# Seven half-sized products in place of eight for the gate groups of three feed-forwards

## What is computed

```python
def first_block(x, ...):
    for l in range(DEPTH):                       # DEPTH = 2
        x = x + 0.5 * swiglu(rmsnorm(x, norm_ffn1[l]), w_ffn1_in[l], w_ffn1_out[l])
        x = x + mixing_sublayer(rmsnorm(x, norm_mix[l]), ...)
        x = x + 0.5 * swiglu(rmsnorm(x, norm_ffn2[l]), w_ffn2_in[l], w_ffn2_out[l])
    return rmsnorm(x, norm_final)
# second block, at its end:
        x = x + jnp.square(jax.nn.relu(hm @ w_mlp_in)) @ w_mlp_out
```

## Time and profile before

| | us |
|---|---|
| time, median of 3 runs | 3125.79 (3125.71 to 3126.05) |
| span of the profiled execution | 3124.5 |
| TensorE busy | 3108.5 |
| VectorE busy | 1536.1 |
| ScalarE busy | 1097.2 |
| GpSimd busy | 253.3 |

### The profile page before, as it was taken

One profiled execution on the slowest core, in us unless ns is written; L12 is line 12 of the kernel. 1 busy time (PEld: TensorE's weight loads), 2 busy tenths in 40 slices (PEclk: granted clock), 3 DMA queues, 4 the chain that ended last, 5 costly groups with the idle time before them and its releaser, 6 DMA issues.

```text
span 3124.5 us, 35882 instructions
## 1 busy us (share of the span) xinstructions
PE 3108.5 (99%) x14334; PEld 2531.9 (81%) x14334; DVE 1536.1 (49%) x2472; ACT 1097.2 (35%) x1536; POOL 253.3 (8%) x223
## 2 busy tenths in 40 slices
PE   9999999999999999999999999999999999999998
PEld 7888887788888888888877788888888877888887
DVE  6434436565443444344456555434556555564352
ACT  5323335333322332233344333322456433332222
POOL 0000104102000010000022011000201000110001
PEclk9999999999999999999999999999999999999999
DMA  5333322222433233333222233233332333333332
GB/s 155 95 96 97 131 88 68 75 81 95 140 96 96 91 105 95 101 95 115 95 75 68 69 105 110 95 95 97 105 107 78 97 96 100 101 95 95 101 94 74
DMA packets 95044, 302.01 MB, mean 97 GB/s; under 512 B 11088, under 2 KB 21456, under 8 KB 94300
## 3 DMA queue, kind: packets, MB, share of 16 engines
q1 hardware_dynamic: 94880, 299.73, 30.8%
HBM read 297.54 MB, written 5.29 MB: 97 GB/s over the span
## 4 chain that ended last, share of the span: by engine, by line
PE 99%; DMA 0%; DVE 0%; ACT 0%; issue 0%; SPq 0%; POOL 0%; POOLq 0%; ACTq 0%; DVEq 0%
PE bank L1657 93%; PE score_ps L1483 1%; PE out_ps L1516 1%; PE turn_ps L1494 1%; PE out_ps L1535 1%; PE score_ps L1525 1%; PE score_ps L1557 1%; PE score_ps L1607 0%; PE turn_ps L1503 0%; PE out_ps L1568 0%; PE turn_ps L1432 0%; PE turn_ps L1414 0%; DMA raw<-w_ffn_in 0%; PE out_ps L1595 0%; PE score_ps L1585 0%; DMA rgw<-rg_in 0%
## 5 line engine op out<-in xcount | busy, mean ns | idle before, releaser
L2075 DVE TENSOR_TENSOR w_lo<-raw,w_hi 128x1024 fp32r<-128x1024 f32 (+1 forms) x548 | 674.5, 1231 | 1188.1 <-ACT w_hi L1689 1187.6
L1657 PE MATMUL bank<-in_hi,w_hi 128*128 128x512 f32 x2704 | 1077.5, 398 | 1.0 <-DVE in_lo L2081 1.0
L1657 PE MATMUL bank<-in_hi,w_lo 128*128 128x512 f32 x2704 | 1054.4, 390 | 0.0
L1657 PE MATMUL bank<-in_lo,w_hi 128*128 128x512 f32 x2704 | 1053.7, 390 | 0.0
L1689 ACT ACTIVATE w_hi<-raw 128x1024 fp32r<-128x1024 f32 (+1 forms) x548 | 567.3, 1037 | 1095.7 <-PE bank L1657 1089.0
L1657 PEld LDWEIGHTS bank<-in_hi,w_hi 128*128 128x128 f32 x2704 | 507.9, 188 | 125.5 <-issue 20.9
L1657 PEld LDWEIGHTS bank<-in_hi,w_lo 128*128 128x128 f32 x2704 | 507.5, 188 | 108.2
L1657 PEld LDWEIGHTS bank<-in_lo,w_hi 128*128 128x128 f32 x2704 | 508.2, 188 | 103.5 <-issue 2.4
L1657 PE MATMUL bank<-hid_hi,w_hi 128*128 128x512 f32 x960 | 373.4, 389 | 0.0
L1657 PE MATMUL bank<-hid_lo,w_hi 128*128 128x512 f32 x960 | 373.4, 389 | 0.0
L1657 PE MATMUL bank<-hid_hi,w_lo 128*128 128x512 f32 x960 | 373.4, 389 | 0.0
(11 more groups left out here) (339 smaller groups left out, 2590.0 us busy)
## 6 DMA issues: line engine op xcount, KB each, us to landing
raw<-w_ffn_in SPq DMA_DIRECT2D x175, 512.0 KB, 3.5
raw<-w_mix SPq DMA_DIRECT2D x90, 512.0 KB, 3.5
raw<-w_ffn_out SPq DMA_DIRECT2D x80, 512.0 KB, 3.5
raw<-w_mixb SPq DMA_DIRECT2D x58, 512.0 KB, 3.6
raw<-w_mlp_in SPq DMA_DIRECT2D x32, 512.0 KB, 3.5
raw<-w_mlp_out SPq DMA_DIRECT2D x32, 512.0 KB, 3.5
raw<-w_w_out SPq DMA_DIRECT2D x16, 512.0 KB, 3.5
raw<-w_ffn_out SPq DMA_DIRECT2D x16, 256.0 KB, 2.7
```

Of the source, the lines that this page charges most:

```text
L1657: mm = pe.matmul(ps, lhs, rhs, start=first and step == 0, stop=last and step == 2, skip_group_check=True)
L2075: dve.tensor_tensor(w_lo[:, i % SPLIT, cut], raw[:, i % RAW, cut], w_hi[:, i % SPLIT, cut].bitcast(F32), ALU.subtract).then_inc(S_["lo_spl ...
```

## The change

A gate group's product, two output tiles by 8 input tiles by 512 tokens, can be seen as a 2 x 2 block product: input tiles in two halves (4 and 4), output tiles in two (1 and 1), tokens in two (LEFT and RIGHT, 256 each). Eight block products are replaced by seven, in the manner of Strassen and Winograd: each of 4 input tiles, one output tile and 256 tokens. For that

- four sums of weight quarters, t1 to t4, are made by VectorE in the raw slots (`st_sum`);
- four combined forms of the activations are made once per feed-forward (`make_forms`) and split in hi and lo, over the first ten beats;
- a group's work becomes four product beats with 2, 2, 1 and 2 products; the first two follow each other at once, the third and fourth come behind the two beats of the plain up group;
- of the running sums in the bank, ScalarE copies four stages out (m1, u2, u3, c21) and VectorE makes three combinations (c11, c22, c12);
- then VectorE multiplies the pair of tiles by the norm factor, and ScalarE takes the silu (`finish_silu`). The up group's eviction is put off, in the list `later`, until that has been filed.

In a product beat's tail `flush` stands ahead of the splits, and `run_later` at the end. `PLAIN_FIRST` leaves plain all groups of ffn1 in layer 0 and of the MLP, the first four in the first piece of the three other feed-forwards, the last two of every piece, and all up groups. That makes gate groups 4, 6, 8 of the first piece and 0, 2, 4, 6 of the second go by seven products: 7 of 22 groups, in three feed-forwards.

PSUM banks are now taken from a queue of free banks, to which score_ps and out_ps are added during such a feed-forward. There are 4 more raw slots for the weights of those groups. The MLP is cut in three pieces (12, 10, 10). `prepare_memory` moves to the start of the last output product of the last feed-forward, and `decay` is loaded in each layer, behind the wait for `gated`. The core of the diff, with empty lines left out:

```diff
-HID = 16
+HID = 12
+QUARTER = UNIT // 2
+LEFT, RIGHT = slice(0, S // 2), slice(S // 2, S)
+FORMS = ("difference", "second", "third", "fourth")
+MORE_RAW = 4
+PLAIN_FIRST = {"ffn1_in0": (12, 10), "ffn2_in0": (4, 0), "ffn1_in1": (4, 0), "ffn2_in1": (4, 0), "mlp_in": (6, 5, 5)}
...
-    half = (n_hidden // 2 + 1) // 2 * 2
-    return [(0, half), (half, n_hidden - half)]
+    n = -(-n_hidden // HID)
+    out, first = [], 0
+    for i in range(n):
+        count = 2 * -(-((n_hidden - first) // 2) // (n - i))
+        out.append((first, count))
+        first += count
+    return out
+def by_products(name, piece, n_groups):
+    return [PLAIN_FIRST[name][piece] <= i < n_groups - 2 and i % 2 == 0 for i in range(n_groups)]
...
+                self.run_later()
+                units = self.units()
+                if self.left:
+                    self.left.popleft()()
...
+    def place_loads(self):
+        slots = [dict(over=None, last=b - RAW, uses=0) for b in range(RAW + MORE_RAW)]
+        for ld in self.loads:
+            if ld["more"]:
+                for s in slots[RAW:]:
+                    if s["last"] < ld["more"] - 1:
+                        s["over"], s["last"] = ("unit_used", ld["more"]), ld["more"] - 1
+            b = min(range(RAW + MORE_RAW if ld["more"] else RAW), key=lambda k: slots[k]["last"])
+            s = slots[b]
+            assert s["last"] < ld["beat"]
+            s["uses"] += 1
+            ld.update(slot=b, over=s["over"], landed=16 * s["uses"])
+            s["over"], s["last"] = ("lo_split", ld["last"] + 1), ld["last"]
...
+    def product_beat(self, pieces, products):
+        i = self.units()
+        beat = dict(i=i, early=[], slots=[], tail=[], pieces=pieces, products=products, load=None, half=None)
+        self.beats.append(beat)
+        self.inp.through = i + 1
+        self.into = beat["tail"]
+        self.flush()
+        self.item("split_hi", i=i + AHEAD)
+        self.item("split_lo", i=i + AHEAD)
+        beat["split_end"] = len(beat["tail"])
+        if self.hooks:
+            self.hooks.popleft()()
+        for fn in self.timed.pop(i, ()):
+            fn()
+        self.run_later()
+        return beat
+    def run_later(self):
+        todo, self.later = self.later, []
+        for fn in todo:
+            fn()
+    def copy_out(self, st, which, units, bank, tile, half):
+        st[which] = self.add("st_copied")
+        self.item("st_copy", st=st, which=which, units=units, bank=bank, tile=tile, half=half)
+    def combine(self, st, which, units, bank, tile, half, copied, op):
+        st[which] = self.add("st_combined")
+        self.item("st_combine", st=st, which=which, units=units, bank=bank, tile=tile, half=half, copied=copied, op=op)
+    def weight_sums(self, st, beat, *names):
+        for which in names:
+            st[which] = self.add("st_sum")
+            beat["tail"].insert(beat["split_end"], dict(kind="st_sum", st=st, which=which))
+            beat["split_end"] += 1
+    def seven_products(self, name, out, finish):
+        if not self.many_banks:
+            self.open_banks()
+        self.groups += 1
+        i = self.units()
+        at = self.cursor.get(name, 0)
+        self.cursor[name] = at + 2 * P * UNIT
+        first, second = [self.load(i, name, at + k * P * UNIT, UNIT, self.stage_start) for k in range(2)]
+        st = dict(first=first, second=second, e0=i, out=out)
+        sums = self.bank_over.take(1)
+        plain = self.bank_over.take(1)
+        self.weight_sums(st, self.beats[-2], "t1", "t2")
+        def product(form, at, bank, start, *waits):
+            return dict(form=form, at=at, bank=bank[0], start=start, waits=waits, st=st,
+                        over=self.bank_over.overs(bank) if start else [], version=self.form_at(form))
+        def piece(at, src, off, ready, n=QUARTER):
+            return dict(at=at, n=n, src=src, off=off, ready=ready)
+        self.product_beat([piece(0, first, 0, None, UNIT)],
+                          [product("left_first", 0, sums, True), product("left_last", QUARTER, plain, True)])
+        def after_first(units=self.units()):
+            self.copy_out(st, "m1", units, sums[0], 0, LEFT)
+            self.combine(st, "c11", units, plain[0], 0, LEFT, "m1", "add")
+            self.bank_over[plain] = ("st_combined", st["c11"])
+        self.waiting.append(after_first)
+        if self.left:
+            self.left.popleft()()
+        self.weight_sums(st, self.beats[-1], "t3", "t4")
+        apart = self.bank_over.take(1)
+        self.product_beat([piece(0, first, 0, "t1"), piece(QUARTER, "t2", 0, "t2")],
+                          [product("difference", 0, apart, True), product("second", QUARTER, sums, False, "m1")])
+        def after_second(units=self.units()):
+            self.copy_out(st, "u2", units, sums[0], 1, LEFT)
+        self.waiting.append(after_second)
+        def third():
+            self.product_beat([piece(0, second, 0, "t3")], [product("third", 0, sums, False, "u2")])
+            def after_third(units=self.units()):
+                self.copy_out(st, "u3", units, sums[0], 1, RIGHT)
+                self.combine(st, "c22", units, apart[0], 1, RIGHT, "u3", "subtract")
+            self.waiting.append(after_third)
+        def fourth():
+            first["last"] = second["last"] = self.units()
+            self.product_beat([piece(0, first, QUARTER, "t4"), piece(QUARTER, second, QUARTER, None)],
+                              [product("right_last", 0, sums, False, "u3"), product("fourth", QUARTER, apart, False, "c22")])
+            def after_fourth(units=self.units()):
+                self.copy_out(st, "c21", units, sums[0], 0, RIGHT)
+                self.bank_over[sums] = ("st_copied", st["c21"])
+                self.combine(st, "c12", units, apart[0], 1, LEFT, "u2", "subtract")
+                self.bank_over[apart] = ("st_combined", st["c12"])
+                self.later.append(lambda: finish(st))
+            self.waiting.append(after_fourth)
+        if self.left:
+            self.left.popleft()()
+        self.left.extend([third, fourth])
...
+                if outs[0][0] - n_hidden in awaiting:
+                    self.later.append(lambda: evict_in(outs, units, pair))
+                    return
...
+            def finish_silu(st, j, awaiting=awaiting):
+                awaiting.remove(j)
+                st["v"], st["silu"] = self.add("dve_evict"), self.add("silu")
+                self.item("finish_silu", st=st, rstd=self.vals["rstd", "rstd"])
+                self.vals["silu", j] = self.vals["silu", j + 1] = st["silu"]
...
+            for tiles, by_seven in zip(groups, seven):
+                if not by_seven:
+                    self.gemm(w_in, DT, [tiles], self.inp, evict_in, fresh=tiles is groups[0])
+                    continue
+                j = tiles[0]
+                in_silu = gated and j < n_hidden or not gated and (j // 2) % 2
+                ring = "silu" if in_silu else "tmp"
+                places = (self.silu if in_silu else self.tmp).take_pair()
+                out = dict(ring=ring, b=places[0].b, places=places, overs=[p.over for p in places if p.over])
+                if gated and j < n_hidden:
+                    held[j], held[j + 1] = places
+                    awaiting.add(j)
+                    self.seven_products(w_in, out, lambda st, j=j: finish_silu(st, j))
...
+            if last and before_last is not None:
+                before_last()
...
-                if it["first"]:
-                    sp.wait_ge(S_["bias_moved"], 16 * 6)
-                    sp.dma_start(decay[:], decay_in).then_inc(S_["decay_loaded"], 16)
                 sp.wait_ge(S_["gated"], it["gated"])
+                sp.dma_start(decay[:], decay_in).then_inc(S_["decay_loaded"], 16)
...
+            def products(b):
+                i = b["i"]
+                pe.wait_ge(S_["lo_split"], i + 1)
+                for part in b["products"]:
+                    for name, value in part["over"]:
+                        pe.wait_ge(S_[name], value)
+                    for which in part["waits"]:
+                        pe.wait_ge(S_["st_combined" if which == "c22" else "st_copied"], part["st"][which])
+                    if formed.get("form_lo", 0) < part["version"]:
+                        formed["form_lo"] = part["version"]
+                        pe.wait_ge(S_["form_lo"], part["version"])
+                    ps = bank[part["bank"]][:, 0:S // 2]
+                    for k in range(TT):
+                        hi, lo = moving(part["form"], k)
+                        at = slice(part["at"] + k * P, part["at"] + (k + 1) * P)
+                        wh, wl = w_hi[:, i % SPLIT, at], w_lo[:, i % SPLIT, at]
+                        for step, (x, y) in enumerate(((hi, wh), (lo, wh), (hi, wl))):
+                            mm = pe.matmul(ps, y, x, start=part["start"] and k == 0 and step == 0,
```

(65 more changed lines are left out.)

305 lines of the change are left out of this document (245 added, 60 removed).

## The result

| | us |
|---|---|
| before, median of 4 runs | 3125.89 (3125.71 to 3126.05) |
| after, median of 4 runs | 3215.59 (3215.25 to 3216.08) |
| ratio | 1.0287 (95% interval 1.0272 to 1.0301) |
| span of the profiled execution | 3213.7 |

A forecast was written before the change was run, and what follows sets the result against it. TensorE, busy 99%, was taken as the bound. 3124.5 - 16.0 (products) + 78 (gaps) + 2 (short waits) + 1 (hidden) + 12 (clock) + 1.3 (to the median) = 3202.8, so 3203 us; 80% in 3160 to 3245.

The forecast's parts named there:

- products and widths: Gate groups by seven: 84 half-wide matmuls replace 48 wide, saving 0.82 us less 0.06 for width switches; 21 groups, 16.0 us gained.
- fifteen gaps: TensorE waits 5.2 us for copy m1 in each seven-group behind an up group whose gate was by seven: 78 us lost.
- three short waits: The first seven-group of each first piece, behind a plain pair, gets m1 0.7 us late, three times: 2 us.
- low clock: TensorE's granted clock may fall in the 5.2 us gaps: 0.8 us a gap in the mean, 12 us.
- hidden parts: Forms, third MLP piece, moved memory tiles and loads: mostly covered, 0 to 5 us in all, 1 us in the sum.
- The chain to m1: Work filed on ScalarE and VectorE ahead of m1 ends m1 at 9.33 us; TensorE, due at 4.3, stands 5.2 us.
- the rival of that name: The clock falls in every gap and stays down afterwards: 1.5 to 4.2 us a gap, 3213 to 3253 us; 20%.
- The signs named: 1764 half-wide matmuls at 0.120 us, 15 waits about 5 us, 3 under 1, two hid_hi before m1, clock below 1.00.
- The faster rival: TensorE does not wait for m1, its copy done 4.32 us after the group's first product beat begins: 3110 us; 11%.
- The shorter wait: Evictions reach VectorE ahead of splits and sums, or mostly so: 1 to 3 us a place, 3130 to 3165; 7%.
- the further wait: TensorE waits again at the first plain or third product beat, as ScalarE and VectorE catch up late: over 3245; 4%.

The follow-up runs named there:

- experiment 2: The change whole, plus sixteen idle 512-column matmuls on TensorE in front of the wait for m1 in the fifteen groups behind a seven-group: 3190.34 us, ratio 1.0206.
- experiment 7: On top of experiment 1, the eviction ahead of a piece's first seven-group is also put off behind its m1: 3110.50 us, ratio 0.9950 to before.
- experiment 4: The change with no group by seven products, leaving the three-piece MLP, moved memory tiles, decay table loaded twice and bank queue: 3127.02 us, ratio 1.0003 to before.
- experiment 1: The change whole, but the last gate group's multiply and silu, and the up group's evict_hidden, are filed later, behind copy m1: 3112.87 us, ratio 0.9959 to before.
- experiment 5: The change whole, but only the up group's evict_hidden is filed behind m1; multiply and silu stay ahead; plain beats take oldest free banks: 3161.77 us, ratio 1.0114.
- experiment 6: The change whole, but the sums t3 and t4 stand behind m1 and c11 in VectorE's order: 3199.80 us, ratio 1.0233 to before.

## Why the prediction was right, step by step

The forecast was 3203 us in a range of 3160 to 3245, slower; measured 3215.6.

| term | predicted | measured | from |
|---|---|---|---|
| products and widths | -16.0 | -15.5 | 7 x 1.44 and two U of 5.47 against four of 5.44: 0.74 x 21 |
| fifteen gaps | 78 | 75 + 1.5 | 5.0 each by the starts; 0.1 each for the restart (experiment 2) |
| three short waits | 2 | 2.2 | 0.6 + 0.1 each; experiment 7 took 2.4 away |
| low clock | 12 | 26 | see below |
| hidden parts | 1 | 0 to 1 | experiment 4 has 1.2, not clear of noise; experiment 7 ends at 15.5 below before, which leaves room for none |
| sum | 77 | 89 to 90 | 89.7 by the medians |

**The saving** came as the windows of before gave it, and not as the 25 us that the prediction estimates from cycle counts: the products still start every 0.120 us, though their operands are other tiles. One figure beside the sum was misread: a half-wide matmul carries 0.120 - 0.2267 / 2 = 0.0067 us beyond half of a wide one, and 0.013 us is the excess of a pair. The 0.82 us doesn't rest on it. The two U beats each show 5.47 between product beats, the 0.03 of the earlier trace rows.

**The chain to m1** went as laid out from the boundary in before, to 0.1 us: with B1 at 831.96, c21 was predicted 0.26 behind it and came at 0.20, w_lo 1.63 (1.56), t3 2.77 (2.70), the multiply 3.99 (3.91), silu 5.26 (5.16), second hid_hi 8.40 (8.37), m1 8.93 (8.91), TensorE's restart 9.4 (9.32). The gap came out at 5.0 + 0.1 us instead of 5.2. That it is the order, and not the sum of the work, is shown by experiment 1; that the length of VectorE's filed work sets the gap by experiments 5 and 6. The first group of a first piece waits 0.6, that of a second piece doesn't: its 48 products from 974.67 took 5.75 us.

**The term that was mis-sized is the clock's price:** 12 us predicted, 26 measured. I took 0.8 us a gap and held that only some gaps would cost it, since the end of before showed "3.9 us with almost no work" ahead of the fall. That stretch is not empty. Behind the last wide matmul TensorE ran sixteen matmuls with one column, and the last of them ended at 3111.87:

```profile
3109.22 0.95 PE L1422 MATMUL turn_ps<-ones,ssum 128*128 128x1 f32 x8
3110.82 1.05 PE L1426 MATMUL turn_ps<-ones,tmp 128*128 128x1 f32 x8 [0.66 <-ACT tmp L1700]
```

TensorE had then stood still for 1.5 us when the clock fell (3113.3), so the row gave no ground for setting a gap of 5.2 us beside it as longer "by a third only". It is also one case only: the change's own falls lie 2.0 to 5.1 us behind the last matmul, and experiment 5 has nine falls at gaps of 2.2 us. The clock fell at every gap of 5.0 us, so the rival of that name (20%) was the truer case: it gave 3213 to 3253, and the forecast's own 3180 to 3213 ends 2.6 us short. The mechanism and the other terms were right; that the total still lies well inside 3160 to 3245 is owed to the wide bounds left for this term. Fifteen times the 12 products and U1 behind a gap took 8.44 to 9.31 us, 8.73 in the mean, against 7.01 with the clock held up: 1.7 us a gap, 26 us in all; experiment 2 gave 25 back.

The page "TensorE: Matmul & The Clock Gate" of the Trainium skill (section "HAM oscillation — how this bites in real kernels") tells of a kernel in which every such wait makes the next burst begin slow. For 5.0 us the trace of after agrees in that all fifteen bursts were slowed, though five began up to 0.3 us before the fall. For gaps of 2.2 us it was nine of fifteen, and each of the nine bursts began at full clock.

**The signs named.** The 1764 matmuls of 256 columns, the fifteen waits of about 5 us and three under 1, and the two hid_hi in front of m1 are all there. The granted clock below 1.00 is seen in windows and in the mean (0.986 against 0.998); the 40 slices of the page read 9 in both kernels.

**The faster rival** (3110 us, 11%) was decided where it said, at the copy m1: experiments 1 and 7 are that rival made true, and end at 3112.9 and 3110.5. The shorter wait and the further wait did not occur: U1 and B3 never waited.

## What to carry to other kernels

Fewer multiplications are worth what the matmul's measured pace gives, here 0.74 us of 10.9 per group; one copy that is filed behind an eviction in an in-order queue can cost nine times that (5.0 + 0.1 + 1.7 us). When a product waits for a small copy on another engine, list what is filed ahead of that copy and what each of those waits for in turn, and put the copy first. A gap in TensorE can cost more than its length, because the clock can fall with it: here it did for all gaps of 3.8 and 5.0 us and for nine of fifteen of 2.2 us, and for none of 0.6 us.

## What the runs showed of the hardware that was not expected

- The granted clock fell to half at nine of fifteen gaps of 2.2 us, and at all of 3.8 us and 5.0 us.
- The fall can come after the work is back: at all nine of the 2.2 us gaps (0.1 to 1.6 us after), at six of fifteen of 3.8 us and at five of fifteen of 5.0 us. Behind the gap of experiment 5 that ends at 837.63, 12 products took 1.54 us, as at full clock, and only U1 was slow (7.07 us for 5.47).
- A shorter gap can cost more clock: 2.0 us in the mean behind 3.8 us, 1.7 us behind 5.0 us.
- With matmuls of no use in the gap and 1.2 us left idle, it fell in none of fifteen.
- The first matmul behind a wait costs 0.10 us more than one in a stream, at full clock.
